# Attention on TensorE: the scores of step n+2 issued behind the values of step n-1 instead of ahead of the transposes of step n

## The chip, the core and the metric

The kernel runs on one NeuronCore of a Trainium2 chip. The metric is the device time of one execution in microseconds (us). The engines are TensorE (PE: matmuls and transposes, reading SBUF and writing PSUM), VectorE (DVE), ScalarE (ACT), GpSimd (POOL) and SyncE (SP, which issues the DMAs). Each engine runs its own instructions in program order, and waits on semaphores where it needs something from another one.

## What is computed

The model is a two-layer hybrid decoder trunk on 1040 positions (16 learned meta tokens and 1024 real ones) with a width of 1024: a Mamba-2 mixer and a convolutional feed-forward net, then sliding-window attention with shared keys and values and a second feed-forward net. The change lies in the attention. Cut to what matters:

```python
def swa_sink_attention(hn, w_q, k, v, sinks, w_o):
    q = (hn @ w_q).reshape(bsz, seq_len, 4, 4, 64) * scale        # 4 key/value heads, 4 query heads for each
    ...
    s_meta = einsum("bnqkgd,bmkd->bnkgqm", qb, km)                # 16 meta keys, always visible
    s_band = einsum("bnqkgd,bnskd->bnkgqs", qb, kband)            # 2 x 128 keys: the block before and its own
    s_band = where(mask, s_band, NEG_INF)
    p = softmax(concatenate([s_meta, s_band, s_sink], -1))        # a sink logit in the denominator
    ob = einsum("...m,bmkd", p[..., :16], vm) + einsum("...s,bnskd", p[..., 16:272], vband)
    return concatenate([om, ob], axis=1) @ w_o
```

## The kernel before

All activations stay in SBUF, transposed (128 channels by 1040 positions). Dense products are made of three f16 matmuls each (lines 1174 to 1176). The attention between them works in f32.

The attention has 36 steps: `QCH` lists the pairs of a query chunk b (chunk 0 holds the 16 meta tokens, chunks 1 to 8 hold 128 tokens each) and a key/value head g, so step n is chunk n // 4 and head n % 4. Steps 0 to 3 have 16 queries and 16 keys, steps 4 to 7 have 128 queries and 144 keys, and the 28 steps from 8 to 35, the "full" steps, have 128 queries and 272 keys. A step handles the 4 query heads of its g together. It passes through four engines:

1. PE, `scores(n)`, line 1468: four score matmuls into PSUM banks 0 to 3. There is one set of these banks, so it first waits for `scores_masked`, which says that DVE has read the scores of step n-1.
2. DVE, `masked(n)`: line 1126 adds the mask and copies the scores into one of three SBUF buffers, line 1129 takes the row maxima, and two small operations (lines 1131 and 1134) prepare the exponent's bias.
3. ACT, `exps(n)`: line 796 four times, and a small one (line 798).
4. DVE, `denominators(n)`: lines 1139 and 1141.
5. POOL, line 453: multiplies the step's probabilities by the reciprocal of the denominator.
6. PE, `transposes(n)`, lines 1481 and 1485, after `probs_normed` (POOL) of step n.
7. ACT, `transposed(n)`, lines 810 and 811: copies the transposed probabilities to SBUF.
8. PE, `values(n)`, lines 1500, 1502 and 1505, after `probs_copied` of step n and after `out_lo_ready` of step n-1 (there is one PSUM bank for the output).
9. ACT, `out_hi(n)`, line 817, and DVE, `out_lo(n)`, line 1145: split the output into two f16 parts, the input of the output projection.

The order on every engine is written out by hand. DVE does this:

```python
            masked(0)
            for n in range(NQD):
                if n + 1 < NQD:
                    masked(n + 1)
                denominators(n)
                if n > 1:
                    out_lo(n - 2)
```

ACT does `transposed(n)`, `exps(n + 2)`, `out_hi(n - 1)` in each turn, after `exps(0)` and `exps(1)`. POOL only normalises, step after step. PE does `scores(n + 2)`, `transposes(n)`, `values(n - 1)` in each turn, after `scores(0)` and `scores(1)`.

Of the kernel before, what the change touches and what calls it, by code (L numbers as in the profile page):

```python
# [79 lines left out]
def program(nc, h0, wa, wd, wdt, prm, out):  # L80
# [4 lines left out]
    with ExitStack() as ctx:  # L85
# [184 lines left out]
        NQD = len(QCH)  # L270

        def keys(b):

            return META if b == 0 else META + P if b == 1 else META + 2 * P
# [17 lines left out]
        def out_t(n):  # L292
            T = CHUNK[QCH[n][0]][1]
            return PS[:, 7, 0:2 * P].rearrange("p (k t) -> p k t", k=2)[:, :, 0:T]
# [871 lines left out]
        def _(eng):  # L1166
# [292 lines left out]
            def scores(n):  # L1459
                b, g = QCH[n]  # L1460
                t0, T = CHUNK[b]
                if n > 0:
                    eng.wait_ge(scores_masked, n)
                for r in range(QPK):
                    hf = slice(64 * (r % 2), 64 * (r % 2) + 64)
                    q_ = QT[2 * g + r // 2][hf, t0:t0 + T]
                    k0 = 0 if b < 2 else MW * (b - 2) + META
                    o = eng.matmul(PS[0:T, r, 0:keys(b)], q_, K2[g][hf, k0:k0 + keys(b)], start=True, stop=True)
                o.then_inc(scores_ready, 1)

            def transposes(n):

                b, g = QCH[n]
                T, sm = CHUNK[b][1], probs(n)
                eng.wait_ge(probs_normed, n + 1)
                if n > 0:
                    eng.wait_ge(probs_copied, n)
                for r in range(QPK):
                    c = ((r % 2) * 2 + r // 2) * P
                    m0 = P if b > 1 else 0  # L1480
                    o = eng.transpose(PS[0:META, 6, c:c + T], sm[:, r, m0:m0 + META], ident[0:T, 0:T])
                    for a in range(2):
                        k0 = m0 + META if a == 1 else 0
                        if b > 1 or (b == 1 and a == 1):
                            o = eng.transpose(PS[:, 4 + a, c:c + P], sm[:, r, k0:k0 + P], ident[:, :])
                o.then_inc(probs_turned, 1)

            def values(n):

                b, g = QCH[n]  # L1490
                T = CHUNK[b][1]
                eng.wait_ge(probs_copied, n + 1)
                if n > 0:
                    eng.wait_ge(out_lo_ready, n)
                kv = slice(g * AD, (g + 1) * AD)
                for hf in range(2):
                    o_ = out_t(n)[64 * hf:64 * hf + 64]
                    c = slice(256 * hf, 256 * hf + 256)
                    pm = PTM[n % 2][0:META, c].rearrange("p (k t) -> p k t", k=2)[:, :, 0:T]
                    o = eng.matmul(o_, VR[0:META, 0, kv], pm, start=True, stop=(b == 0))  # L1500
                    if b > 1:
                        eng.matmul(o_, VR[:, b - 1, kv], PTS[n % 2][:, c].rearrange("p (k t) -> p k t", k=2),
                                   start=False, stop=False)
                    if b > 0:
                        o = eng.matmul(o_, VR[:, b, kv], PTS[n % 2][:, 512:1024][:, c].rearrange("p (k t) -> p k t", k=2),
                                       start=False, stop=True)
                o.then_inc(values_ready, 1)
# [2 lines left out]
            scores(0)  # L1510
            scores(1)
            for n in range(NQD):
                if n + 2 < NQD:
                    scores(n + 2)
                transposes(n)
                if n > 0:
                    values(n - 1)
            values(NQD - 1)

            eng.wait_ge(out_lo_ready, NQD)  # L1520
# [77 lines left out]
```

## Time and profile before

| | |
|---|---|
| device time, three runs | 3048.89, 3055.19, 3057.05 us (median 3055.19) |
| span of the profiled execution | 3056.2 us, 45646 instructions |
| PE busy | 2787.8 us, 91% of the span |
| DVE, ACT, POOL busy | 1487.5, 946.0, 673.9 us (49%, 31%, 22%) |
| the attention's steps | from 1963.97 us (first scores) to about 2190 us |

The page gives the profiled execution's span and no device time of its own beside it; the span lies 1.0 us above the median of the three runs. Times in rows are microseconds from the start of the span. A row of the timeline has the start, the duration, the engine, the line, the operation, what it writes and reads, and in brackets how long the engine had been idle and who released it. The stage of the attention is where PE waits for other engines step by step; before and after it PE runs through dense products.

### The profile page before, as it was taken

Reading aid. Unit: us, or ns where it says so; the run is one execution under the profiler, and the core shown is the slowest. Engines: PE = TensorE matmul, PEld = TensorE weight load, DVE = VectorE, ACT = ScalarE, POOL = GpSimd, SP = SyncE. Lnnn points to the kernel's source line nnn. Section 1 sums busy time; section 2 is a strip of 40 time slices with the busy share of each in tenths; the row PEclk is TensorE's granted clock in tenths of the full one; section 3 lists DMA queues with packets and bytes.
Section 4 is the critical chain, followed back from the end, with each engine's and each line's share of the span. In section 5 each row is a group of like instructions: output and inputs, shape, how many; then the busy total and the mean of one; then the engine's idle time right before and its main releaser. Section 6 shows DMA issues by size and latency. Waiting matters only on the chain.

```text
span 3056.2 us, 45646 instructions
## 1 busy us (share of the span) xinstructions
PE 2787.8 (91%) x17830; PEld 1810.3 (59%) x17830; DVE 1487.5 (49%) x1715; ACT 946.0 (31%) x1676; POOL 673.9 (22%) x463
## 2 busy tenths in 40 slices
PE   6989899897789799999999979899997999999996
PEld 4655566564456466666666645545564666666664
DVE  5565665666651555555521173255346555554113
ACT  4321212223231333333321144356434333332111
POOL 1031140412443401011021240023252101011124
PEclk8999999898999899999999989889998999999998
DMA  2100101000011011111111101100010111111111
GB/s 97 49 28 22 42 15 43 21 28 28 1 35 48 14 53 50 48 48 48 60 48 57 42 14 42 41 1 1 8 42 28 48 48 51 52 48 55 56 47 55
DMA packets 34864, 119.50 MB, mean 39 GB/s; under 512 B 3265, under 2 KB 9537, under 8 KB 34753
## 3 DMA queue, kind: packets, MB, share of 16 engines
q1 hardware_dynamic: 34752, 117.99, 12.1%
q8 instruction: 74, 1.21, 0.2%
q14 instruction: 38, 0.30, 0.0%
HBM read 113.78 MB, written 4.19 MB: 39 GB/s over the span
## 4 chain that ended last, share of the span: by engine, by line
PE 70%; DVE 14%; ACT 6%; issue 3%; DVEq 3%; POOL 2%; ACTq 1%; DMA 0%; POOLq 0%; SPq 0%
PE PS L1174 21%; PE PS L1175 21%; PE PS L1176 21%; DVE TT L978 3%; DVE wlo L859 2%; DVE UB L877 2%; PE PS L1403 2%; ACT whi L469 1%; DVEq L1128 1%; ACT TT L796 1%; DVE small L1129 1%; DVE R L866 1%; POOL hT L422 1%; PE PS L1408 1%; POOL TT L365 1%
## 5 line engine op out<-in xcount | busy, mean ns | idle before, releaser
L1174 PE MATMUL PS<-R,whi 128*128 128x384 f16 (+1 forms) x3360 | 1053.6, 314 | 35.6 <-DVE wlo L859 13.1
L1175 PE MATMUL PS<-R,whi 128*128 128x384 f16 (+1 forms) x3360 | 1053.0, 313 | 0.0
L1176 PE MATMUL PS<-R,wlo 128*128 128x384 f16 (+1 forms) x3360 | 1052.6, 313 | 0.0
L859 DVE SCALAR_TENSOR_TENSOR wlo<-stage,whi 128x1408 f16<-128x1408 f32 x196 | 338.1, 1726 | 1089.9 <-ACT whi L469 1089.9
L1174 PE MATMUL PS<-BIG,whi 128*128 128x384 f16 (+1 forms) x1632 | 511.2, 313 | 29.6 <-DVE BIG L1082 16.2
L1176 PE MATMUL PS<-BIG,wlo 128*128 128x384 f16 (+1 forms) x1632 | 511.2, 313 | 0.0
L1175 PE MATMUL PS<-BIG,whi 128*128 128x384 f16 (+1 forms) x1632 | 511.2, 313 | 0.0
L1174 PEld LDWEIGHTS PS<-R,whi 128*128 128x128 f16 x3360 | 332.2, 99 | 214.0 <-issue 36.8
L1175 PEld LDWEIGHTS PS<-R,whi 128*128 128x128 f16 x3360 | 332.0, 99 | 173.1 <-issue 11.8
L1176 PEld LDWEIGHTS PS<-R,wlo 128*128 128x128 f16 x3360 | 332.0, 99 | 169.7 <-issue 3.6
L978 DVE SCALAR_TENSOR_TENSOR TT<-UB,pr,TT 128x1040 f32<-128x1040 f32 x248 | 327.3, 1320 | 43.1 <-issue 41.7
L469 ACT ACTIVATE whi<-stage 128x1408 f16<-128x1408 f32 x196 | 269.2, 1375 | 215.3 <-PE PS L1176 215.3
L428 POOL TENSOR_TENSOR BIG<-TT,BIG 128x1040 f32 x44 | 95.1, 2160 | 854.3 <-ACT BIG L748 854.3
L1174 PEld LDWEIGHTS PS<-BIG,whi 128*128 128x128 f16 x1632 | 161.1, 99 | 117.7 <-DVE wlo L859 12.1
L1176 PEld LDWEIGHTS PS<-BIG,wlo 128*128 128x128 f16 x1632 | 161.2, 99 | 82.1 <-issue 1.0
L1175 PEld LDWEIGHTS PS<-BIG,whi 128*128 128x128 f16 x1632 | 161.1, 99 | 81.3 <-issue 1.2
L365 POOL TENSOR_TENSOR TT<-AUX,upper 128x1024 f16<-128x1024 f32 (+3 forms) x72 | 131.7, 1849 | 331.8 <-PE PS L1356 310.2
L479 ACT ACTIVATE UB<-PS 128x272 f32<-128x272 f32 x348 | 139.3, 451 | 119.4 <-PE PS L1176 110.7
L748 ACT ACTIVATE BIG<-TT 128x1040 f32 x44 | 47.1, 1070 | 322.8 <-DVE TT L1101 322.8
L403 POOL TENSOR_TENSOR TT<-R 128x384 f32 (+1 forms) x63 | 46.5, 763 | 397.7 <-ACT R L479 397.7
L746 ACT ACTIVATE TT<-TT 128x1040 f32<-128x1040 f32 x44 | 47.1, 1070 | 253.5 <-DVE TT L978 253.5
L479 ACT ACTIVATE R<-PS 128x384 f32 (+3 forms) x72 | 32.6, 458 | 261.3 <-PE PS L1176 259.1
(191 smaller groups left out, 2725.7 us busy)
## 6 DMA issues: line engine op xcount, KB each, us to landing
stage<-wa SPq DMA_DIRECT2D x164, 512.0 KB, 3.5
stage<-wd SPq DMA_DIRECT2D x32, 704.0 KB, 4.0
hT<-h SPq DMA_DIRECT2D x2, 1536.0 KB, 11.1
out<-hT SPq DMA_DIRECT2D x2, 1536.0 KB, 5.8
hT<-h SPq DMA_DIRECT2D x1, 1088.0 KB, 5.6
out<-hT SPq DMA_DIRECT2D x1, 1024.0 KB, 4.6
pr<-prm SPq DMA_DIRECT2D x1, 328.0 KB, 5.6
BIG<-wdt SPq DMA_DIRECT2D x1, 128.0 KB, 12.0
```

The costliest lines, as they stand in the source:

```text
L365: r = eng.tensor_tensor(aU[part][0:T, 0:HG * T].rearrange("p (h l) -> p h l", h=HG), ar_p[part][0:T, ds(g * HG + c * NH, HG)].unsqueeze(2) ...
L428: eng.tensor_tensor(BIGh[:, ds(t, 1), L:2 * L], T2, BIGh[:, ds(t, 1), 0:L], ALU.subtract).then_inc(hid_lo, 1)
L469: eng.activation(whi[:, slot, :], stage[:, slot, :], ACT.Copy, scale=WS).then_inc(w_hi, 1)
L479: r = eng.activation(dst, PS[:, 3 * st_ + b, 0:n], ACT.Copy, scale=scale)
L746: eng.activation(T0, T0, ACT.Silu).then_inc(act_f, 1)
L859: eng.scalar_tensor_tensor(out=wlo[:, slot, :], in0=stage[:, slot, :], scalar=WS, in1=whi[:, slot, :], op0=ALU.mult, op1=ALU.subtract).the ...
L877: eng.scalar_tensor_tensor(out=ring(i % 6, n), in0=hT[:, k, s:s + n], scalar=prc(C_PRE[v] + k), in1=T1[:, s:s + n], op0=ALU.mult, op1=ALU. ...
L978: r = eng.scalar_tensor_tensor(out=dst, in0=UB[:, s_, o:o + L], scalar=prc(col + k), in1=dst, op0=ALU.mult, op1=ALU.add)
L1174: eng.matmul(acc, whi[:, slot, ws], x(0, k, b), start=first, stop=False)
L1175: eng.matmul(acc, whi[:, slot, ws], x(1, k, b), start=False, stop=False)
L1176: return eng.matmul(acc, wlo[:, slot, ws], x(0, k, b), start=False, stop=last)
L1403: r = eng.matmul(PS[0:T, 7, h * HD:(h + 1) * HD], Em[0:T, h * T:(h + 1) * T], xdt[0:T, h * HD:(h + 1) * HD], start=True, stop=True)
```

## The change

In PE's loop the call of `scores(n + 2)` is moved from the head of the turn to its end:

```diff
             scores(0)
             scores(1)
             for n in range(NQD):
-                if n + 2 < NQD:
-                    scores(n + 2)
                 transposes(n)
                 if n > 0:
                     values(n - 1)
+                if n + 2 < NQD:
+                    scores(n + 2)
             values(NQD - 1)
```

No instruction is added or removed, and the order on DVE, ACT, POOL and SP is the same. Below is the first piece of the difference on PE, at the start of the attention (L1468 are scores, L1481 transposes, L1500 values; `16x16` scores are those of steps 0 to 3; the waits are named in brackets):

```order
 L1468 MATMUL PS<-BIG 16x16 [waits scores_masked]
 L1468 MATMUL PS<-BIG 16x16 x3
-L1468 MATMUL PS<-BIG 16x16 [waits scores_masked]
-L1468 MATMUL PS<-BIG 16x16 x3
 L1481 MATMUL PS<-ident,TT 16x16 [waits probs_normed]
 L1481 MATMUL PS<-ident,TT 16x16 x3
```

The scores of step 2 stood ahead of the transposes of step 0 and now stand behind them. In the middle of the program the kinds of instructions alternate as before, scores, transposes, values, and only the step to which a group of scores belongs has changed. It can be seen where the number of keys changes, here between `values(4)` (L1500, L1505) and `transposes(6)` (L1481, L1485); `128x144` are scores of steps 4 to 7, `128x272` of step 8 and later:

```order
 L1500 MATMUL PS<-UB,AUX 64x256
 L1505 MATMUL PS<-UB,AUX 64x256
-L1468 MATMUL PS<-BIG 128x272 [waits scores_masked]
-L1468 MATMUL PS<-BIG 128x272 x3
+L1468 MATMUL PS<-BIG 128x144 [waits scores_masked]
+L1468 MATMUL PS<-BIG 128x144 x3
 L1481 MATMUL PS<-ident,TT 16x128 [waits probs_copied,probs_normed]
 L1485 MATMUL PS<-ident,TT 128x128
```

Before, `scores(8)` stood here; now it is `scores(7)`, and `scores(8)` comes one group of transposes and values later. So each group of scores from step 2 on is issued behind one more group of transposes and one more group of values.

## Rows read from the trace of the kernel before

**Rows 1.** Waits of engines between 2030 and 2153 us: total, times, longest.

```profile
DVE R L1145 <- ACT R L817: 45.2, 20, 2.3
```

**Rows 2.** Timeline of one full step, 2061 to 2069 us.

```profile
2061.34 1.28 DVE L1126 TENSOR_TENSOR TT<-PS,AUX 128x1088 f32<-128x1088 f32 x1
...
2062.28 0.64 PE L1500 MATMUL PS<-UB,AUX 16*64 16x256 f32 x2
...
2064.54 0.52 ACT L796 ACTIVATE TT<-TT,small 128x272 f32<-128x272 f32 x1 [0.66 <-DVEq L1135]
...
2065.10 2.00 POOL L453 TENSOR_TENSOR BIG<-BIG,small 128x1088 f32<-128x1088 f32 x1 [4.28 <-DVE small L1141]
...
2065.44 1.19 PE L1468 MATMUL PS<-BIG 64*128 64x272 f32 x8
...
2067.15 0.09 PEld L1481 LDWEIGHTS PS<-ident,BIG 128*16 128x16 f32 x1 [0.95 <-POOL BIG L453]
...
2067.28 0.42 DVE L1145 TENSOR_TENSOR R<-PS,R 128x256 f16<-128x256 f32 x1 [2.26 <-ACT R L817]
...
2067.62 1.28 DVE L1126 TENSOR_TENSOR TT<-PS,AUX 128x1088 f32<-128x1088 f32 x1
...
2068.56 0.64 PE L1500 MATMUL PS<-UB,AUX 16*64 16x256 f32 x2
```

**Rows 3.** Windows: busy time per engine, then PE's granted clock, DMA share, GB/s.

```profile
2008.00:2018.20 10.20, 10.20 (x35) 5.54 (x35) 5.29 (x9) 4.10 (x13) 2.00 (x1) 0.50 0.00 0
2154.00:2185.50 31.50, 27.25 (x148) 14.79 (x148) 12.25 (x26) 17.55 (x49) 9.47 (x5) 1.00 0.00 1
2185.60:2195.60 10.00, 8.79 (x30) 4.34 (x29) 0.42 (x1) 0.38 (x1) 0.96 (x1) 0.50 0.00 0
2195.80:2200.00 4.20, 4.20 (x29) 2.60 (x27) 0.00 (x0) 0.40 (x1) 0.64 (x1) 1.00 0.02 4
```

**Rows 4.** Timeline of full steps at the lower clock, 2007 to 2017 us.

```profile
2007.91 0.31 PE L1481 MATMUL PS<-ident,BIG 128*16 128x128 f32 x1 [2.50 <-POOL BIG L453]
...
2008.38 1.28 DVE L1126 TENSOR_TENSOR TT<-PS,AUX 128x1088 f32<-128x1088 f32 x1
...
2010.50 1.11 PE L1500 MATMUL PS<-UB,AUX 16*64 16x256 f32 x2
...
2014.67 2.19 PE L1468 MATMUL PS<-BIG 64*128 64x272 f32 x8
...
2016.90 1.29 DVE L1126 TENSOR_TENSOR BIG<-PS,AUX 128x1088 f32<-128x1088 f32 x1 [1.29 <-PE PS L1468]
```

**Rows 5.** Timeline of the last steps and the first tile behind them.

```profile
2168.55 1.28 DVE L1126 TENSOR_TENSOR BIG<-PS,AUX 128x1088 f32<-128x1088 f32 x1
...
2184.59 0.61 PE L1500 MATMUL PS<-UB,AUX 16*64 16x256 f32 x2 [1.02 <-DVE R L1145]
...
2187.73 1.12 PE L1502 MATMUL PS<-AUX 128*64 128x256 f32 x2
2188.64 1.06 PE L1505 MATMUL PS<-AUX 128*64 128x256 f32 x2
...
2190.91 0.40 PE L1174 MATMUL PS<-R,whi 128*128 128x272 f16 x1 [1.21 <-DVE R L1145]
```

**Rows 6.** Timeline of the first steps, 1969 to 1994 us.

```profile
1969.51 0.18 DVE L1126 TENSOR_TENSOR BIG<-PS,AUX 16x64 f32<-16x64 f32 x1
...
1981.66 1.15 POOL L453 TENSOR_TENSOR TT<-TT,small 128x576 f32<-128x576 f32 x1 [4.10 <-DVE small L1141]
...
1982.86 0.38 PE L1481 MATMUL PS<-ident,TT 128*16 128x128 f32 x1 [1.76 <-POOL TT L453]
...
1984.67 0.42 PE L1500 MATMUL PS<-UB,AUX 16*64 16x32 f32 x4
1985.02 1.33 PE L1468 MATMUL PS<-BIG 64*128 64x144 f32 x8
...
1989.03 1.11 PE L1500 MATMUL PS<-UB,AUX 16*64 16x256 f32 x2
```

## The prediction

> **What bounds the kernel now.** I read the page first: PE is 91% busy, so most of the span is dense products that the change doesn't touch. Then the waits in the attention's steady part, then the timeline of one step, then the clock of the stage by windows.
>
> The waits give the loop away: in twenty full steps DVE stood 45.2 us at line 1145, 2.26 each, for ACT's line 817 [rows 1]. The timeline says what the period is made of. Call the start of a step's mask (line 1126) M. From M of step n+2 at 2061.34 it is 3.20 us until ACT begins its exponentials (2064.54), 2.74 until `out_lo` (2067.28), which is the exponentials and `out_hi`, and 0.34 until the next M at 2067.62: 6.28 us, all of it on DVE and ACT [rows 2]. The reader is to see that PE is not in this circle. Its scores for the M at 2067.62 start at 2065.44 and last 1.19 us, so they are there at 2066.63, 1.0 us early [rows 2]. PE does 3.15 us of values (2062.28 to 2065.43), about 1.2 of scores and 1.41 of transposes (2067.15 to 2068.56), 5.75 of each 6.28 us [rows 2], and its clock is at the full level, 1.00 [rows 3].
>
> What matters is which step's scores are those 1.0 us early ones. The transposes at 2067.15 belong to step n+1 (POOL normalised it from 2065.10 on), and the scores ahead of them to step n+3 [rows 2]. They don't depend on the transposes behind them.
>
> **The change.** It removes and adds no instruction and no DMA; every queue but PE's keeps its order. Each group of scores is moved past one group of transposes and one of values. The moved matmuls cost what they cost. The moved wait, `scores_masked`, is satisfied long before. What changes is what the scores now stand behind: `transposes(n+1)` waits for POOL's step n+1, which waits for `denominators(n+1)`, and that stands on DVE right behind `masked(n+2)`. Behind the late scores then wait DVE's M, everything queued behind it, and through the denominators the next transposes. So a circle closes that did not exist:
>
> M of step k+1, denominators of k, POOL k, transposes k, values k-1, scores k+2, M of step k+2.
>
> Two steps of lead have become one, and nothing in the circle lies beside anything else in it. Its terms at the full clock: M to POOL's start 3.76 (2061.34 to 2065.10), POOL's start to the transposes 2.05 (to 2067.15), transposes 1.41, values 3.15, scores to M: the group's 1.19 and a few hundredths, 1.25 [rows 2]. The sum is 11.62 us instead of 6.28. The old circle of 6.28 stays hidden inside it: `out_lo` of two steps back is done 6.36 after M (its start at 5.94 and 0.42), and the values that wait for it start at 3.76 + 2.05 + 1.41 = 7.22.
>
> **The clock.** PE would now work 5.75 of 11.6 us and stand the other 5.8 in one piece. In this very stage, 2.50 us of standing before 2007.91 was enough: the transposes behind it ran slow, and from 2008.0 to 2018.2 the granted clock is 0.50 [rows 3, 4], which is 1.2 GHz instead of 2.4. PE was busy all through those 10.2 us, with one group each of transposes, values, scores and transposes, before the clock came back. Likewise it fell at the stage's end and stayed at 0.50 from 2185.6 on, through values at full occupancy [rows 3, 5]. A burst here is one group of each kind, about 11 us at the lower level, then 5.8 us of standing. So I take the lower level for every burst.
>
> At that level the transposes of a full step take 2.59 (2007.91 to 2010.50) and scores to M 2.23 (2014.67 to 2016.90) [rows 4]. The values of step 7 or earlier, which lack line 1502, take 4.17 (2010.50 to 2014.67) [rows 4]; the two pairs of line 1502 add 2 x 0.91 (2187.73 to 2188.64) [rows 5], and I take 5.9, less a little overlap. The circle is then 3.76 + 2.05 + 2.59 + 5.9 + 2.23 = 16.53 us.
>
> The Trainium skill, page "TensorE: Matmul & The Clock Gate", section "HAM oscillation — how this bites in real kernels", speaks against this change: waits between bursts of matmuls let the clock drop, so that each burst starts cold. By that the circle can't be the 11.62 of the full clock, and the row at 2007.91 agrees. But its section "What's actually happening" lets sustained activity release the clock again, without naming a kind of matmul; by that a burst of 11 us would finish fast. The 10.2 us at 0.50 with PE busy speak for a later return in f32 work. That is the second rival below.
>
> **The sum.** I count from M to M.
>
> - Start of the stage, M of step 2 to M of step 10. Before: 1969.51 to 2008.38, 38.9 us [rows 4, 6]. After, M of step 2 comes about 1.0 later, behind transposes(0). Then the circles, lower clock throughout as before: for k = 1 to 3 small groups, about 2.8, 3.9 and 4.95 (my estimate from the neighbouring rows, with the first 144-key scores of 1.4 in the last two). For k = 4: 2.66 from M to POOL, 1.20 to the transposes (1981.66 to 1982.86), 1.81 transposes (to 1984.67), 0.35 small values (to 1985.02), scores 1.4: 7.4 [rows 6]. For k = 5 the values are 4.17 (they start at 1989.03 in that stage): 11.25. For k = 6 the scores are 2.23: 12.1. For k = 7 M to POOL is 3.76: 13.2. For k = 8 POOL and transposes are those of a full step: 14.8. Together 71.4, so M of step 10 falls at 2040.9 instead of 2008.38: +32.5.
> - Full circles, k = 9 to 33, 25 of them. Before: 2008.38 to 2168.55, 160.2 us [rows 4, 5]. After: 25 x 16.53 = 413.3. +253.1.
> - The end, last M to the first tile of the output projection. Before: 2168.55 to 2190.91, 22.4 [rows 5]. After: 5.81 to the transposes, then 2.59, 5.9, 2.59, 5.9, 1.1 for `out_lo` (1.02 before 2184.59 [rows 5]), 5.9, and 1.2 for the last split: 31.0. +8.7.
>
> The sum is +294. The profiled span of 3056.2 becomes 3350.5; it lay 1 us above the median, so the predicted time is **3350 us**. A miss of 0.3 in the circle moves it by 8.
>
> **The rivals.**
>
> *The clock stays full, or nearly (0.03).* For it: the duty of PE is that of no row here, 50%. Against it: every stand of 2.5 us and more in the stage was followed by 0.50. The full circles are then 25 x 11.62 = 290.5 instead of 413.3, and start and end lose some 20 more: 3207 us.
>
> *The clock comes back inside each burst (0.14).* For it: behind the stage f16 tiles started at 2190.91 at the low clock, which lasted to 2195.6 and was 1.00 from 2195.8 on [rows 3, 5]: 4.7 us of work. Against it are the 10.2 us of f32 work. If it came after 4.7 us: transposes 2.59, values 2.1 at the low level (36% of them), 2.0 at the full, scores 1.25; the circle is 13.75, and 25 x 2.8 = 70 us come off: 3280.
>
> *Not slower, even faster (0.03).* In the stretches at the lower clock the transposes wait behind the scores: at 2014.67 PE could have turned the probabilities, and it did scores for 2.1 us first. Issued first, transposes feed ACT sooner. If the transposes, copies and values set the pace this would bring up to 2.1 us at three places and nothing elsewhere, 3049. It decides only if the scores had a slack of over 5.3 us (11.62 - 6.28) before their M; they have 1.0, and at 2016.90 DVE was released by the scores themselves after 1.29 us of idling [rows 4]. I keep 0.03 for a dependence read wrong.
>
> *Forecast: the circle at the lower clock, 0.80*, of which a tenth may miss its size.
>
> **Range and chances.** The forecast's own range is 3335 to 3370 (the circle at 16.53 -0.5/+0.6, the end's clock). Down to 3275 it takes in the clock's return inside the burst; it leaves out the full clock and the faster case. Up to 3370 it allows a circle 0.8 longer. A difference of 0.3%, 9 us, is what the measurement can tell; only the last rival lies within or below it: faster 0.01, same 0.02, slower 0.97.
>
> **What the profile of after would show.** DVE line 1126 waits for PE line 1468 in every full step, some 10 us each; the wait of line 1145 for ACT 817 (45.2 us in twenty steps) stays about 2.3 a step. M to M is 16.5, or 13.8, or 11.6, which tells the three clock cases apart; the windows of the stage show a clock of 0.5 in the bursts. PE's transposes are released by POOL after some 5.8 us of standing. POOL's start follows M by 3.76 as before. The dense products before and behind the stage keep their durations. I would be wrong if DVE's mask were not waiting for scores, or if the clock were 1.00 inside bursts.

## The result and the profile after

The changed kernel takes 3331.72 us (median of 4 runs, 3320.76 to 3334.84) against 3052.22 us before (4 runs): a ratio of 1.0911 with a 95% interval of 1.0889 to 1.0933. The profiled execution has a span of 3319.0 us, 262.8 more than before; it is the fastest of the four (3320.76, the others 3331.66 to 3334.84), and the sums below are those of this execution. The forecast was 3350 us in a range of 3275 to 3370, slower with a chance of 0.97.

The page after, its first rows and the row of the clock in 40 slices:

```profile
span 3319.0 us, 45646 instructions
...
PE 2888.6 (87%) x17830; PEld 1856.2 (56%) x17830; DVE 1490.5 (45%) x1715; ACT 946.5 (29%) x1676; POOL 674.5 (20%) x463
...
PEclk8989898989998999999998986566579999999998
```

The same 45646 instructions. PE was busy for 100.8 us more with the same work; in the attention alone it was 303.0 us instead of 195.6, at the lower clock of the slices 25 to 30.

The waits of the changed kernel between 2100 and 2400 us (total, times, longest):

```profile
DVE TT L1126 <- PE PS L1468: 122.1, 13, 10.2
...
DVE BIG L1126 <- PE PS L1468: 64.6, 7, 10.2
...
DVE R L1145 <- ACT R L817: 43.0, 19, 2.3
```

On DVE a wait now leads that the full steps before had only at the low clock (1.29 us at 2016.90, [rows 4]): the mask's for PE's scores, 186.7 us in twenty waits, up to 10.2 each. The old wait of line 1145 is still there, 2.26 a step as in [rows 1], and no longer sets the pace. One circle of the changed kernel in the timeline:

```profile
2099.47 1.29 DVE L1126 TENSOR_TENSOR BIG<-PS,AUX 128x1088 f32<-128x1088 f32 x1 [10.21 <-PE PS L1468]
...
2103.23 2.00 POOL L453 TENSOR_TENSOR TT<-TT,small 128x1088 f32<-128x1088 f32 x1 [14.58 <-DVE small L1141]
...
2105.28 0.38 PE L1481 MATMUL PS<-ident,TT 128*16 128x128 f32 x1 [5.86 <-POOL TT L453]
...
2107.94 1.11 PE L1500 MATMUL PS<-UB,AUX 16*64 16x256 f32 x2
...
2113.82 2.19 PE L1468 MATMUL PS<-BIG 64*128 64x272 f32 x8
...
2116.05 1.29 DVE L1126 TENSOR_TENSOR TT<-PS,AUX 128x1088 f32<-128x1088 f32 x1 [10.22 <-PE PS L1468]
```

From mask to mask it is 16.58 us: 3.76 to POOL, 2.05 to the transposes, 2.66 of transposes, 5.88 of values, 2.23 to the next mask. The forecast had 3.76, 2.05, 2.59, 5.9 and 2.23, together 16.53. But not every circle is like this one. From the mask of step 10 to that of step 35 there are 25, and 7 of them take 12.9 to 13.3 us. Here is one:

```profile
2040.08 1.29 DVE L1126 TENSOR_TENSOR TT<-PS,AUX 128x1088 f32<-128x1088 f32 x1 [8.51 <-PE PS L1468]
...
2045.90 0.38 PE L1481 MATMUL PS<-ident,TT 128*16 128x128 f32 x1 [5.87 <-POOL TT L453]
...
2048.56 0.70 PE L1500 MATMUL PS<-UB,AUX 16*64 16x256 f32 x2
...
2051.77 1.19 PE L1468 MATMUL PS<-BIG 64*128 64x272 f32 x8
...
2053.01 1.29 DVE L1126 TENSOR_TENSOR BIG<-PS,AUX 128x1088 f32<-128x1088 f32 x1 [6.55 <-PE PS L1468]
```

The transposes run at the low clock (2.66 us), but the values take only 3.21 and the scores 1.24: the clock came back between the two. The windows show the same in the next burst, first within its values, and then a row of four circles with no such return (the third number from the right is the granted clock):

```profile
2061.50:2062.30 0.80, 0.80 (x3) 0.26 (x2) 0.00 (x0) 0.71 (x1) 0.00 (x0) 0.50 0.00 0
2062.50:2066.20 3.70, 3.70 (x19) 1.77 (x18) 0.00 (x0) 0.58 (x2) 0.00 (x0) 1.00 0.00 0
```

```profile
2082.90:2149.20 66.30, 42.88 (x128) 21.40 (x128) 14.66 (x28) 16.39 (x48) 8.00 (x4) 0.53 0.00 0
```

The 0.53 is 0.50 from 2087 on. In the first 3.3 us the clock was 1.00, but there PE stood: it had come back as the burst before ended, too late to shorten anything.

The stage's start and end:

```profile
1966.92 0.21 DVE L1126 TENSOR_TENSOR BIG<-PS,AUX 16x64 f32<-16x64 f32 x1 [0.96 <-PE PS L1468]
...
2430.55 1.29 DVE L1126 TENSOR_TENSOR BIG<-PS,AUX 128x1088 f32<-128x1088 f32 x1 [10.21 <-PE PS L1468]
...
2456.46 0.29 PE L1174 MATMUL PS<-R,whi 128*128 128x272 f16 x1 [1.21 <-DVE R L1145]
```

```profile
2455.00:2460.50 5.50, 4.29 (x34) 3.15 (x33) 0.42 (x1) 0.78 (x2) 1.35 (x2) 1.00 0.00 0
```

The account by the forecast's three terms: masks 2 to 10, 73.2 us (1966.92 to 2040.08) instead of 38.9, +34.3 (the forecast's +32.5 is +31.5 for this stretch and 1.0 for a later mask 2); the 25 full circles, 390.5 instead of 160.2, +230.3 (forecast +253.1); the end, 25.9 instead of 22.4, +3.5 (forecast +8.7). The sum is 268.1. Mask 2 stands 2.6 us earlier than before, because the whole attention began earlier in this execution (its first mask at 1963.13 instead of 1966.75); counted from that first mask it comes 1.0 later, as forecast. Behind the stage the first f16 tiles had the full clock (before: 0.50 up to 2195.6, [rows 3]). That gives back 2.4: the first tile lies 265.6 us behind that of before, those from 2459 to 2484 only 263.2. What comes after takes another 0.4 off: 262.8.

### The profile page after: what moved, and what is told of

Read it like the earlier page. It is cut to its first block, busy times and chain, and to the rows that moved or that the text cites. A ratio compares the mean times of both kernels' runs of the same rounds, so it can differ in the third digit from the quotient of the medians.

```text
span 3319.0 us, 45646 instructions
## 1 busy us (share of the span) xinstructions
PE 2888.6 (87%) x17830; PEld 1856.2 (56%) x17830; DVE 1490.5 (45%) x1715; ACT 946.5 (29%) x1676; POOL 674.5 (20%) x463
## 4 chain that ended last, share of the span: by engine, by line
PE 72%; DVE 15%; ACT 4%; POOL 4%; issue 3%; DVEq 1%; ACTq 0%; DMA 0%; POOLq 0%; SPq 0%
PE PS L1174 19%; PE PS L1175 19%; PE PS L1176 19%; DVE TT L978 2%; PE PS L1500 2%; DVE wlo L859 2%; DVE UB L877 2%; PE PS L1468 2%; PE PS L1403 2%; PE PS L1485 2%; PE PS L1502 2%; PE PS L1505 1%; ACT whi L469 1%; POOL TT L453 1%; DVE small L1129 1%
## 5 line engine op out<-in xcount | busy, mean ns | idle before, releaser
L1174 PE MATMUL PS<-R,whi 128*128 128x384 f16 (+1 forms) x3360 | 1052.6, 313 | 35.8 <-issue 13.2
L1481 PE MATMUL PS<-ident,TT 128*16 128x128 f32 (+1 forms) x96 | 35.2, 382 | 126.6 <-POOL TT L453 126.6
```

The costliest lines, as they stand in the source:

```text
L1174: eng.matmul(acc, whi[:, slot, ws], x(0, k, b), start=first, stop=False)
```

## The experiments

Theory: the late scores close a circle (mask, denominators, POOL, transposes, values, scores, mask), and its idle time takes the clock down. Rivals: only TensorE's own time ahead of the scores counts, in whatever order DVE works; or the loss is the clock's alone; or the clock plays no part. Each ratio below is to the kernel before, run on the same chip, with its 95% interval.

**e1: half of the move.** The scores stand between transposes and values. The edit is shown against the changed kernel:

```diff
                 transposes(n)
-                if n > 0:
-                    values(n - 1)
                 if n + 2 < NQD:
                     scores(n + 2)
+                if n > 0:
+                    values(n - 1)
```

> Half of the move: the scores of step n+2 stand behind the transposes of step n but ahead of the values of step n-1. Theory (a closed circle mask, denominators, POOL, transposes, scores, mask): the values drop out of the circle, which is 3.76 + 2.05 + 1.41 + 1.25 = 8.5 us at the full clock; at the low clock TensorE has 2.59 + 2.19 + 5.9 = 10.7 us of work per step and no idle time, so the clock should come back: a mix of 8.5 and 10.7 us per step, about 3135 us (3105 to 3175). Rival (only TensorE's own time ahead of the scores counts, less the 1.0 us that they were early; no circle): 1.41 - 1.0 = 0.4 us per step, about 3065 us.

Measured: 3161.11 us, 1.0358 (1.0341 to 1.0376). In the timeline of this kernel:

```profile
2120.65 1.29 DVE L1126 TENSOR_TENSOR BIG<-PS,AUX 128x1088 f32<-128x1088 f32 x1 [3.71 <-PE PS L1468]
...
2126.47 0.28 PE L1481 MATMUL PS<-ident,TT 128*16 128x128 f32 x1 [2.71 <-POOL TT L453]
...
2128.90 1.79 PE L1468 MATMUL PS<-BIG 64*128 64x272 f32 x8
...
2130.74 1.29 DVE L1126 TENSOR_TENSOR TT<-PS,AUX 128x1088 f32<-128x1088 f32 x1 [3.72 <-PE PS L1468]
```

The values have left the circle: 5.82 us to the transposes, 2.43 of transposes, 1.84 to the next mask. The period is 10.1 us in most of the full steps (8.5 to 10.5 over all of them). The rival's 3065 us is out. The forecast of 3135 was a little low, inside its range of 3105 to 3175: the clock does fall and return, but within each burst, so the 8.5 us of the full clock are seen once.

**e2 and e3: the order on DVE.** The same edit in the changed kernel (e2) and in the one before (e3):

```diff
             for n in range(NQD):
+                denominators(n)
                 if n + 1 < NQD:
                     masked(n + 1)
-                denominators(n)
```

> The changed kernel, and on DVE denominators(n) stands ahead of masked(n+1) instead of behind it. Theory: the circle of one step is cut, since the denominators no longer wait behind a mask that waits for the scores. What is left goes through two steps: mask 3.2, exponentials 2.3, denominators 0.5, POOL 2.1, transposes 1.4, values 3.15, scores 1.25, about 14 us for two steps or 7.0 each, and DVE's own chain is about 6.8. Some 25 to 45 us above the kernel before: 3080 to 3100 us. Rival (the late scores cost what they cost on TensorE, whatever the order on DVE): no change against 3332 us.

> The control of the run before: the same swap on DVE in the kernel before. DVE's chain becomes about 6.8 us per full step (denominators 0.5 behind out_lo, ahead of the mask) instead of 6.28: 3065 to 3070 us. Theory: the move of the scores costs 10 to 35 us on top of this kernel, against 280 on top of the kernel before. Rival: 280 us here too.

Measured: e2 3289.7 us, 1.0792 (1.0774 to 1.0810); e3 3063.19 us, 1.0042 (1.0025 to 1.0059), a period of 6.62 us. The control came within 2 us of what was expected (3065 to 3070). e2 did not. Against the ratio of 1.0911 it gains 1.2 points, some 36 us, neither 240 nor nothing; and on top of e3, with the same order on DVE, the late scores still cost some 227 us, where 10 to 35 were expected. Its timeline shows why:

```profile
2138.35 1.29 DVE L1126 TENSOR_TENSOR BIG<-PS,AUX 128x1088 f32<-128x1088 f32 x1 [7.91 <-PE PS L1468]
...
2141.56 0.52 ACT L796 ACTIVATE BIG<-BIG,small 128x272 f32<-128x272 f32 x1 [10.52 <-DVEq L1135]
...
2143.88 0.38 ACT L817 ACTIVATE R<-PS 128x256 f16<-128x256 f32 x1
...
2144.30 0.43 DVE L1145 TENSOR_TENSOR R<-PS,R 128x256 f16<-128x256 f32 x1 [2.80 <-ACT R L817]
...
2144.87 1.08 PE L1500 MATMUL PS<-UB,AUX 16*64 16x256 f32 x2 [5.08 <-DVE R L1145]
...
2150.72 1.84 PE L1468 MATMUL PS<-BIG 64*128 64x272 f32 x8
...
2152.61 1.29 DVE L1126 TENSOR_TENSOR TT<-PS,AUX 128x1088 f32<-128x1088 f32 x1 [7.57 <-PE PS L1468]
```

PE no longer waits for POOL but for `out_lo` (line 1145). A second circle runs through the late scores: mask, exponentials, `out_hi`, `out_lo`, values, scores, mask. It takes 14.2 to 14.6 us, with the values at the low clock; in the changed kernel it was hidden under the 16.6 of the first. So e2 shows that the first circle set the pace, and that cutting it alone wins only the difference.

**e8 and e9: both circles cut.** In the changed kernel (e8) and in the one before (e9); the comment lines name the engine's part of the kernel:

```diff
 # DVE
             for n in range(NQD):
-                if n + 1 < NQD:
-                    masked(n + 1)
                 denominators(n)
                 if n > 1:
                     out_lo(n - 2)
+                if n + 1 < NQD:
+                    masked(n + 1)
 # ACT
                 transposed(n)
-                if n + 2 < NQD:
-                    exps(n + 2)
                 if n > 0:
                     out_hi(n - 1)
+                if n + 2 < NQD:
+                    exps(n + 2)
```

> The changed order on TensorE, with both circles through the late scores cut. Run e2 cut the first, and a second one of 14.6 us came out: mask, exponentials, out_hi, out_lo, values, scores, mask. Here DVE does denominators(n), out_lo(n-2), masked(n+1) in this order and ACT does out_hi(n-1) ahead of exps(n+2), so that no values wait for something behind the mask just started. Revised theory: what is left takes two steps for one turn (mask to exponentials' end 5.6, denominators 0.4, POOL 2.1, transposes 1.4, values 3.15, scores 1.25: 13.9), 7.0 us per step at the full clock: 3075 to 3100 us. Rival (scores behind values are slow whatever stands elsewhere): above 3250 us.

> The control of e8: the same new orders on DVE and ACT with TensorE's order of before. Theory: DVE's chain mask, exponentials, denominators, out_lo, mask is 3.2 + 2.3 + 0.5 + 0.4, about 6.3 to 6.4 us per full step, as before: 3048 to 3058 us.

Measured: e8 3118.73 us, 1.0216 (1.0199 to 1.0233); e9 3145.45 us, 1.0308 (1.0294 to 1.0322). With the same order on TensorE that cost 9% above, e8 is only 2% above the kernel before: what makes the late scores dear is what stands around them. Both are slower than expected (3075 to 3100 and 3048 to 3058), and these rows of e8 tell what I had left out:

```profile
2125.09 1.28 DVE L1126 TENSOR_TENSOR BIG<-PS,AUX 128x1088 f32<-128x1088 f32 x1
...
2130.66 1.02 ACT L810 ACTIVATE UB<-PS 128x1024 f32<-128x1024 f32 x1 [0.16 <-issue]
...
2132.25 0.38 ACT L817 ACTIVATE R<-PS 128x256 f16<-128x256 f32 x1
2132.67 0.42 DVE L1145 TENSOR_TENSOR R<-PS,R 128x256 f16<-128x256 f32 x1 [1.69 <-ACT R L817]
2133.01 1.28 DVE L1126 TENSOR_TENSOR TT<-PS,AUX 128x1088 f32<-128x1088 f32 x1
```

ACT's copies of the transposed probabilities (1.6 us) now stand between the exponentials and `out_hi`, and the next mask behind `out_lo`: 7.92 us, on DVE and ACT alone. That is the period of 19 of the 25 full steps; the other six take 9.7 to 10.7, with the low clock in them. And e9, with the early scores, is the slower of the two. In its timeline:

```profile
2127.82 2.00 POOL L453 TENSOR_TENSOR TT<-TT,small 128x1088 f32<-128x1088 f32 x1 [9.76 <-DVE small L1141]
...
2131.22 1.28 DVE L1126 TENSOR_TENSOR TT<-PS,AUX 128x1088 f32<-128x1088 f32 x1
...
2132.55 1.63 PE L1468 MATMUL PS<-BIG 64*128 64x272 f32 x8 [2.13 <-DVE TT L1126]
...
2134.11 0.38 PE L1481 MATMUL PS<-ident,TT 128*16 128x128 f32 x1
```

Where DVE's mask is late, the early scores wait on PE for their PSUM banks, 2.13 us, and the transposes, whose probabilities POOL had finished at 2129.82, stand behind them and start at 2134.11. This is the mechanism of the rival on the other side: with these orders on DVE and ACT the move gains 0.9% (1.0216 over 1.0308, both to the kernel before). How much of that is the order alone and how much the low clock, which e9 has somewhat more of, is not separated. In the kernel before, the scores' waits were satisfied, so there was nothing to gain.

**e4: the clock.** Extra f16 matmuls in PE's idle time from step 8 on, in the changed kernel, 60 and then 95 of them:

```diff
             for n in range(NQD):
+                if n > 7:
+                    eng.wait_ge(probs_copied, n)
+                    for _ in range(60):
+                        eng.matmul(PS[:, 4, 0:P], lower16[:, :], lower16[:, :], start=True, stop=True)
                 transposes(n)
```

> The changed kernel, with 60 extra f16 matmuls of 128 columns ahead of the transposes of each step from 8 on, into a PSUM bank that the transposes then overwrite, so that TensorE works through most of the 5.8 us in which it waits for POOL. The output is the reference's. Theory: the clock stays at its full level, the extra matmuls (3.4 us at that level) fit into the wait, and the circle is 11.6 us: about 3210 us (3195 to 3235). The part above the kernel before, some 155 us, is then the dependence alone, and the other 120 us of the 280 are the clock. Rival A (the loss is the clock's alone, the order costs nothing at the full clock): near 3055 us. Rival B (the clock plays no part): 3332 us or more.

> As e4_fill, with 95 extra matmuls instead of 60. With 60, TensorE still stood 2.4 us per step and the clock fell in half of the steps; 95 take 95 x 0.0587 = 5.6 us at the full clock and fill the wait of 5.8 us. Theory: the clock stays full in every step, every full circle is 11.62 us: about 3205 us (3195 to 3225). Rival (the extra matmuls themselves lengthen the circle, or the clock falls all the same): 3270 us or more.

Measured: with 60, 3278.84 us, 1.0746 (1.0728 to 1.0764), above the 3195 to 3235 expected; with 95, 3220.18 us, 1.0550 (1.0533 to 1.0568), as expected. With 60 the circle at the full clock is there, exactly as summed, in 11 of 25 steps (11 more take 15.4 to 16.5, three 13.2):

```profile
2137.55 1.29 DVE L1126 TENSOR_TENSOR BIG<-PS,AUX 128x1088 f32<-128x1088 f32 x1 [5.24 <-PE PS L1468]
...
2143.36 0.28 PE L1481 MATMUL PS<-ident,TT 128*16 128x128 f32 x1 [2.41 <-POOL TT L453]
...
2149.16 1.29 DVE L1126 TENSOR_TENSOR TT<-PS,AUX 128x1088 f32<-128x1088 f32 x1 [5.24 <-PE PS L1468]
```

PE still stood 2.41 us per step, and the clock fell in the 14 longer circles. With 95 it stands 0.45, and the window over the last 24 of the 25 circles has a clock of 1.00:

```profile
2047.46:2326.61 279.15, 267.89 (x3050) 203.54 (x3049) 88.01 (x168) 98.35 (x288) 47.99 (x24) 1.00 0.01 2
```

That is 11.63 us a circle against the 11.62 forecast for the full clock. PE is 96% busy here and the kernel is slower than before by 5.5%: a busy PE proves nothing. The rivals are out: at the full clock the order still costs far more than nothing (3055 us), and the clock does play a part (3332 us or more). The dependence costs up to 5.5%, 167 us; the clock adds at least the other 3.6 points, about 110 us. The split isn't sharper because the steps ahead of step 8 have no extra matmuls and kept their low clock. In the 25 full circles alone the traces give +130.6 us for the dependence (290.8 instead of 160.2) and 99.7 more for the clock.

**e5 and e6: POOL as a link.** POOL normalises one head of four; the other three are left unnormalised, so a part of the computation is left out, and only the time is of interest. In the changed kernel (e5) and in the one before (e6):

```diff
-                eng.tensor_tensor(probs(n), probs(n), soft(n, 4).unsqueeze(2).broadcast_to([T, QPK, w]),
-                                  ALU.mult).then_inc(probs_normed, 1)
+                eng.tensor_tensor(probs(n)[:, 0:1, :], probs(n)[:, 0:1, :],
+                                  soft(n, 4)[:, 0:1].unsqueeze(2).broadcast_to([T, 1, w]),
+                                  ALU.mult).then_inc(probs_normed, 1)
```

> The changed kernel, and POOL normalises only one of the four heads of a step (the other three stay unnormalised: a part of the computation is left out), so that its 2.0 us become about 0.55. Theory (POOL is a link of the circle): each circle is some 1.45 us shorter, 15.1 instead of 16.6 at the low clock: 3285 to 3300 us. Rival (the late scores cost only TensorE's own time): no change against 3332 us.

> The control of e5: the same short POOL operation in the kernel before (three of four heads are left unnormalised), where POOL is in no circle. Theory: within 0.3% of the kernel before. Rival (POOL sets the pace in both kernels): 40 us less.

Measured: e5 3284.48 us, 1.0754 (1.0736 to 1.0772), e6 3050.16 us, 0.9987 (0.9977 to 0.9997). Both came as expected. The circle of e5 (the edit adds a line, so the lines behind it have numbers one higher):

```profile
2125.52 1.29 DVE L1127 TENSOR_TENSOR TT<-PS,AUX 128x1088 f32<-128x1088 f32 x1 [8.86 <-PE PS L1469]
...
2129.28 0.64 POOL L453 TENSOR_TENSOR TT<-TT,small 128x272 f32<-128x272 f32 x1 [14.59 <-DVE small L1142]
...
2140.75 1.29 DVE L1127 TENSOR_TENSOR BIG<-PS,AUX 128x1088 f32<-128x1088 f32 x1 [8.86 <-PE PS L1469]
```

15.23 us instead of 16.59: 1.36 less, which is what POOL gave up (2.00 to 0.64). In the kernel before the same cut moves the time by 0.1%. POOL is a link of the new circle and of none before.

**e7 and e10: `out_hi` ahead of the exponentials.** The ACT part of the edit of e8 alone, in the kernel before (e7) and in the changed one (e10).

> The kernel before, and on ACT out_hi(n-1) stands ahead of exps(n+2) instead of behind it. The circle of 6.28 us (mask, exponentials, out_hi, out_lo, mask) is cut, since out_lo no longer waits for the exponentials. TensorE then has 5.75 us of work per step, and ACT's own chain (transposed, a wait for the values, out_hi, exps) about 5.95. Theory: 5.95 to 6.1 us per full step, 5 to 9 us off: about 3043 us. Rival (ACT now waits for the values and delays the exponentials, which were early): no gain or up to 10 us more.

> The changed kernel with the order on ACT that gained 0.8% in the kernel before (out_hi(n-1) ahead of exps(n+2)). It cuts the second circle (mask, exponentials, out_hi, out_lo, values, scores) and leaves the first (mask, denominators, POOL, transposes, values, scores). Theory: the first alone sets the pace of the changed kernel and the second lies hidden in it, so nothing changes: 3320 to 3340 us. Rival (the second circle is part of the loss): 20 us or more below 3332.

Measured: e7 3030.88 us, 0.9924 (0.9911 to 0.9938), 12 us less than expected; e10 3319.59 us, 1.0876 (1.0858 to 1.0894). e7 is the fastest of all, 22 us below the kernel before. Some 14 us of it lie in the 25 full steps (145.8 instead of 160.2) and some 10 in the steps from 2 to 10 (28.4 instead of 38.9), which the expectation had left out. In its timeline:

```profile
2101.41 0.38 ACT L817 ACTIVATE R<-PS 128x256 f16<-128x256 f32 x1 [1.55 <-PE PS L1505]
...
2101.83 0.42 DVE L1145 TENSOR_TENSOR R<-PS,R 128x256 f16<-128x256 f32 x1 [1.30 <-ACT R L817]
...
2102.54 1.29 DVE L1126 TENSOR_TENSOR TT<-PS,AUX 128x1088 f32<-128x1088 f32 x1 [0.29 <-PE PS L1468]
...
2108.47 1.29 DVE L1126 TENSOR_TENSOR BIG<-PS,AUX 128x1088 f32<-128x1088 f32 x1 [0.29 <-PE PS L1468]
```

The circle of 6.28 that bound the kernel before is cut. Masks follow each other by 5.69 and 5.93 us in turn, and now wait 0.29 for scores: PE, with its 5.75 us of work, has become the bound (91.5 of 93.3 us busy from 2050 to 2143), so the slack of 1.0 us is used up. In e10 the full circles are 16.59 as without the edit (6 of 25 near 13), so the second circle is hidden in the full steps. Its median lies 12 us under the changed kernel's, at the edge of what I expected, and the two intervals overlap. Some 2.3 us of it I can place: between the masks of steps 3 and 5 two periods shrank from 4.78 and 6.34 to 3.83 and 4.95, since there the second circle is the longer one. The rest is not explained; the two profiled executions, the fastest of either kernel, lie only 2.4 us apart.

## Why the prediction was right

The mechanism was right and one term too large. The measured 3331.72 us lie 3 below the forecast's own range of 3335 to 3370, and inside the full range only because that was drawn down to 3275 for a clock that comes back.

- **What bound the kernel before**, the circle of 6.28 us on DVE and ACT: shown by e7, where cutting it brought the full steps from 6.28 to 5.8 us and the kernel 0.8% down.
- **The new circle and its terms**: shown. 11.62 forecast and 11.63 measured at the full clock (e4 with 95); at the low clock 16.53 forecast, 16.59 measured; POOL's part by e5 and e6; the denominators behind the mask by e2 against e3; the values' part by e1.
- **The clock**: right for 18 of the 25 circles. In the other 7 it came back within the burst, which the forecast had as a rival for all of them at 13.75 us each; measured were 12.9 to 13.3. This is the mis-sized term: the full circles cost +230.3 instead of +253.1, and the end, where it also came back, +3.5 instead of +8.7. The step that failed is the one from the 10.2 us of f32 work at 0.50 [rows 3, 4] to "the lower level for every burst". That one stretch was not the rule: behind the transposes of 2045.90 the clock was back after 2.7 us. The return may also be why the four executions differ by 14 us among themselves, against 8 before. The traced one is the fastest and has the highest mean clock (0.904, the others 0.900 to 0.902), so the others may well have fewer returns; there is the trace of one only.
- **The start.** Counted from the first mask, mask 10 came 35.3 us later than before, 2.8 more than the forecast's +32.5. Of that, 2.3 are the circles of k = 2 and 3, estimated at 3.9 and 4.95 and measured at 4.78 and 6.34. e10, which cuts the second circle, has 3.83 and 4.95 there: the estimate lacked that circle.
- **The Trainium skill** says in "TensorE: Matmul & The Clock Gate", section "HAM oscillation — how this bites in real kernels", that bursts behind waits start cold. The trace agrees in every one of the 25 full circles: the transposes take 2.65 or 2.66 us, against 1.41 at the full clock. The section "What's actually happening" lets sustained activity release the clock; here that shortened the burst in 7 of the 25.
- **The old circle "hidden inside"**: right for the full steps of the changed kernel, and incomplete. The forecast saw that the values wait for `out_lo` with 0.86 us to spare, but not that values and scores make this a second circle of 14.6 us. It made the expectation for e2 wrong by 190 us.
- **The other sign**: rightly given little here. The rows of e9 show that the mechanism exists, where the mask is late and the early scores hold up the transposes.

## What to carry to other kernels

Before moving work behind a wait on an in-order engine, follow what that wait depends on through every other queue, in queue order too, until it comes back to the moved work or doesn't. If it comes back, all terms of the circle add up, whatever each engine's busy share, and there may be a second circle right under the first. A step of lead less is not dear in itself: with one step of lead the kernel was 9% slower, and 2% where the orders on DVE and ACT left neither circle closed. Add the clock: the circle left TensorE idle in one piece, and here that made 5.5% into 9%.

## What the runs showed of the hardware that was not expected

The return of TensorE's clock in f32 work is not a matter of the burst's length alone. Bursts that began alike, with a group of f32 transposes after 5.87 us of standing, had the full clock again after 2.7 us in one circle and in others not through the transposes and 8 us of values and scores. They are not scattered: in this execution they are circles 1 and 2, 8, 15 and 16, 22 and 23 of the 25, about every seventh (in e10: 4 and 5, 12, 18 and 19, 25). So something regular in time may tell them apart, and not what the burst holds; no run tests it, and it is open. And 2.41 us of standing per step, with f16 matmuls for 3.5 us ahead of it, brought the clock down in 14 of the 25 circles (e4 with 60). Long standing isn't needed either: in the kernel before, the clock was 1.00 up to 2185.5 and 0.50 behind it [rows 3], with PE at work since a stand of 1.02 us that ended at 2184.59 [rows 5].
